# Start addresses modulo 256 of the split weights and of the streamed tiles, in a two-block fp32 network

## The reference

```python
h = rms_norm(x, norm1_g) @ w_in                      # 2048 -> 6176
x = x + concat([gla(h), windowed_attention(h)]) @ w_out
xt = rms_norm(x, norm2_g); idx, gates = topk(xt @ w_query, sub_keys)
x = x + sum_k(gates * gelu(expert_down[idx] . xt) * expert_up[idx])
for i in range(2):
    u, z = split(rmsnorm(x) @ w_in_2[i])             # 2048 -> 2 x 4096
    y = (pool_mixer(u) if i == 0 else rglru(conv(u))) * silu(z)
    x = x + rmsnorm(y @ w_out_2[i])                  # 4096 -> 2048
    x = x + rmsnorm((p[i] @ w_ple[i]) * sigmoid(rmsnorm(x) @ w_ple_gate[i]))
```

## Time and profile before

| | |
|---|---|
| median of the timed runs | 3753.89 us (3752.56 to 3755.21, 2 runs) |
| the profiled execution | 3742.33 us, span 3741.0 us |
| granted TensorE clock, mean of the profiled execution | 0.974 of full speed |
| busy: PE, DVE, ACT, POOL | 94%, 64%, 43%, 13% of the span |
| moved by DMA | 668.69 MB, 179 GB/s on average |

### The profile page before, as it was taken

The page is one execution under the profiler, slowest core; times in us unless marked ns, Lnnn a source line. Parts: engine busy times, 40 slices in busy tenths (PEclk is TensorE's granted clock), DMA queues, the critical chain, the costliest instruction groups (busy, mean ns, idle before and its releaser), DMA issues.

```text
span 3741.0 us, 67022 instructions
## 1 busy us (share of the span) xinstructions
PE 3532.1 (94%) x29266; PEld 3474.5 (93%) x29266; DVE 2396.2 (64%) x3293; ACT 1624.0 (43%) x1770; POOL 478.9 (13%) x420
## 2 busy tenths in 40 slices
PE   7999899999899998999999999999998798988987
PEld 7899899999899998999999899999998798988987
DVE  5676579874445556555555777777446777876465
ACT  3444333454444444544344543333444354555343
POOL 1000100397920000000000100000004200000013
PEclk9999999999999999999999999999998799999989
DMA  5434455455456666555666645555553344444533
GB/s 203 147 136 158 144 207 181 181 192 193 185 205 210 210 210 169 203 197 192 208 209 210 162 172 192 192 192 194 190 181 136 115 170 159 174 164 164 186 124 136
DMA packets 140388, 668.69 MB, mean 179 GB/s; under 512 B 10752, under 2 KB 60672, under 8 KB 78528
## 3 DMA queue, kind: packets, MB, share of 16 engines
q1 hardware_dynamic: 103184, 622.65, 48.1%
q10 hardware_dynamic: 36912, 41.75, 3.3%
HBM read 643.39 MB, written 20.97 MB: 178 GB/s over the span
## 4 chain that ended last, share of the span: by engine, by line
PE 77%; DVE 14%; ACT 5%; issue 4%; DMA 1%; POOL 0%; SPq 0%; ACTq 0%; DVEq 0%
PE PS L441 24%; PE PS L442 24%; PE PS L443 24%; DVE WL L1313 4%; ACT WH L887 3%; PE PS L701 1%; DVE A L1333 1%; DVE UCS L1900 1%; DVE A L1331 1%; DVE CO L1660 1%; DVE OO L1820 1%; DVE EE L1848 1%; ACT XT L1056 0%; DMA RAW<-in_w_in 0%; DVE XT L1822 0%
## 5 line engine op out<-in xcount | busy, mean ns | idle before, releaser
L1313 DVE TENSOR_TENSOR WL<-RAW,WH 128x2048 fp32r<-128x2048 f32 (+2 forms) x653 | 1359.9, 2083 | 943.3 <-ACT WH L887 942.6
L441 PE MATMUL PS<-A,WH 128*128 128x256 f32 x5648 | 1621.1, 287 | 100.0 <-DVE WL L1313 59.4
L442 PE MATMUL PS<-A,WH 128*128 128x256 f32 x5648 | 1590.6, 282 | 0.0
L443 PE MATMUL PS<-A,WL 128*128 128x256 f32 x5648 | 1590.3, 282 | 0.0
L887 ACT ACTIVATE WH<-RAW 128x2048 fp32r<-128x2048 f32 (+2 forms) x653 | 1136.6, 1743 | 851.5 <-PE PS L443 820.7
L441 PEld LDWEIGHTS PS<-A,WH 128*128 128x128 f32 x5648 | 1083.0, 192 | 132.2 <-issue 79.4
L442 PEld LDWEIGHTS PS<-A,WH 128*128 128x128 f32 x5648 | 1083.7, 192 | 3.9 <-issue 2.9
L443 PEld LDWEIGHTS PS<-A,WL 128*128 128x128 f32 x5648 | 1084.6, 192 | 0.0
L441 PE MATMUL PS<-CO,WH 128*128 128x256 f32 x2048 | 578.0, 282 | 30.8 <-DVE CO L1660 29.3
L443 PE MATMUL PS<-CO,WL 128*128 128x256 f32 x2048 | 575.0, 281 | 0.0
L442 PE MATMUL PS<-CO,WH 128*128 128x256 f32 x2048 | 574.2, 280 | 0.0
(11 more groups left out here) (236 smaller groups left out, 3180.9 us busy)
## 6 DMA issues: line engine op xcount, KB each, us to landing
RAW<-in_w_in SPq DMA_DIRECT2D x177, 1024.0 KB, 4.8
RAW<-in_peer_down SPq DMA_DIRECT2D x128, 1024.0 KB, 4.8
RAW<-in_peer_up SPq DMA_DIRECT2D x128, 896.0 KB, 5.0
RAW<-in_w_out SPq DMA_DIRECT2D x80, 1024.0 KB, 4.7
RAW<-in_w_gate SPq DMA_DIRECT2D x32, 1024.0 KB, 4.7
RAW<-in_w_query SPq DMA_DIRECT2D x16, 1024.0 KB, 4.8
gates_away<-XT ACTq DMA_DIRECT2D x16, 1024.0 KB, 4.0
RAW<-in_peer_up SPq DMA_DIRECT2D x16, 1024.0 KB, 11.0
```

The lines of the kernel that those rows point to most:

```text
L441: e.matmul(ps, wh, x[:, k, 0, :], start=first, stop=False, skip_group_check=True)
L442: e.matmul(ps, wh, x[:, k, 1, :], start=False, stop=False, skip_group_check=True)
L443: return e.matmul(ps, wl, x[:, k, 0, :], start=False, stop=last, skip_group_check=True)
L1313: ins = e.tensor_tensor(WL[:, s, cs], RAW[:, r, cs], WH[:, s, cs].bitcast(F32), ALU.subtract)
```

## The change

WH and WL are no longer one tile of three places each but six tiles. A new helper, `put_at`, places each at a given value modulo 256; where that is no multiple of 32 it places a tile that begins a few elements earlier and uses it from there on. The 64 bytes that were left out ahead of RAW are gone, and what follows the weights moves by 352 bytes. `block`, `hi` and `lo` index the lists.

```diff
     place["at"] += 64
     A = put("A", [128, KD, 2, T], FR)
-    place["at"] += 64
     RAW = put("RAW", [128, NRAW, 2048])
-    WH = put("WH", [128, NSPL, 2048], FR)
-    WL = put("WL", [128, NSPL, 2048], FR)
+
+    def put_at(name, phase):
+
+        place["at"] += (phase - place["at"]) % 256
+        skip = place["at"] % 32 // 4
+        place["at"] -= 4 * skip
+        return put(name, [128, 2048 + skip], FR)[:, skip:skip + 2048]
+
+    WH, WL = [None] * NSPL, [None] * NSPL
+    WH[0], WH[1] = put_at("WH0", 0), put_at("WH1", 64)
+    WL[0], WL[1] = put_at("WL0", 64), put_at("WL1", 64)
+    WH[2], WL[2] = put_at("WH2", 80), put_at("WL2", 80)
...
-        wh, wl = WH[:, s, b * 128:b * 128 + 128], WL[:, s, b * 128:b * 128 + 128]
+        wh, wl = WH[s][:, b * 128:b * 128 + 128], WL[s][:, b * 128:b * 128 + 128]
...
-        ins = e.activation(WH[:, s, q * n:q * n + n], RAW[:, r, q * n:q * n + n], ACT.Copy)
+        ins = e.activation(WH[s][:, q * n:q * n + n], RAW[:, r, q * n:q * n + n], ACT.Copy)
...
-        ins = e.tensor_tensor(WL[:, s, cs], RAW[:, r, cs], WH[:, s, cs].bitcast(F32), ALU.subtract)
+        ins = e.tensor_tensor(WL[s][:, cs], RAW[:, r, cs], WH[s][:, cs].bitcast(F32), ALU.subtract)
```

## The result

The changed kernel takes 3796.28 us (3795.13 to 3797.44, 2 runs) against 3753.89 before: 1.0113 times as long, interval 1.0069 to 1.0156. It is slower by 1.1%; 3689 was forecast.

What follows compares the result with a forecast made beforehand. TensorE's matmul spacing was taken as the bound. From the 3753.9 us median, 56 us plus 16 us came off, giving 3682; with a tenth of matmuls still slow the gain was 65 us, 3689, range 3620 to 3800.

Steps and rivals of the forecast that it cites:

- What bounds the kernel: Whole kernel: limited by how fast matmuls follow one another, with TensorE busy 94% of the 3741.0 us span.
- The reading that the distance decides: All block matmuls: stream start relative to weights decides possible spacings; 192 allows 113.3 and 117.77 ns, 64 only the slow one.
- Step 1: Block matmuls: the new stream-minus-weights distances, 80 to 192, were all priced at 113.3 ns.
- The bounds: Spacing limits for the unseen distances: 108.5 ns from transposes below, 117.77 ns as the longest unbroken spacing above.
- Step 2: Matmuls gaining on the path: 56 us from 12,566 slow ones plus 16 us from broken stages; 72 us, bounds 56 to 103.
- the third for the broken stages: Stages where TensorE waits: 10,530 matmuls could gain 0 to 47 us; a third was taken, 16 us.
- Steps 3 to 5: High/low splits stay covered, RAW's move costs 0, small tiles at 32 or 160 cost 0, with 7 us kept in range.
- R3: Rival, chance 0.11: 112 and 128 behave as 64, A loses its fast spacing; +39 us, 3793.
- R4: Rival, chance 0.11: weight load and moving read collide at mixed or 16-byte distances, another 4.45 ns step; +126 us, 3880.
- R1: Rival, chance 0.23: restarts set the spacing, or new distances are slow as often as old; 3754, give or take 12.

Runs made afterwards that it cites:

- distances alone: Bare kernel without the network: 512 stretches of 48 matmuls over all pairs of weight and stream starts in 16-byte steps; 113.3 ns at distance 192.

## Why the prediction was wrong

- **What bounds the kernel** held: TensorE's spacing. Nothing else moved, and 61 us more of busy TensorE became 53 us of span.
- **The reading that the distance decides** held; it is now shown (distances alone; everything 64 further; all streams at 192).
- **Step 1 failed: "I take 113.3, because it is the nearest row to a distance that is no longer 64."** The trace showed two distances, and nothing in it ordered the others. I treated 64 as a bad exception and everything else as good. It is the reverse: 192 is one of two good ones (112 the other, and only with weights at even multiples of 16), and the other distances have medians from 115.8 to 120.2 ns. A, which had the 192, now has 128 in place 1 and 112 with weights at 80 in place 2, and in the measurement of distances these cost 118.6 and 120.0 ns against 113.3; the other streams went from 64 (117.8) to 96 (120.0) in place 1 and to 80 (118.1) in place 2. In the kernel that is 3.6 ns more for each matmul on A and 1.0 for each other one, where 4.45 ns less were priced for every long one. The bounds were too narrow as well: "no longer spacing holds in any unbroken stretch" is true of the trace and says nothing about pairs that it does not hold.
- **Step 2 was right in size.** It priced all at 113.3 with 72 us off the median, 3682; the kernel that brings nearly all there is 69 us below the one before beside it, at 3682.4. That the two times agree to a microsecond is luck: the third for the broken stages was a choice, and the starting medians differ by 2 us. The step also says that DVE is busy two thirds or less in the unbroken slow windows but for 512 to 706; from 1470 to 1516 it is busy 41.79 of 46 us, which bears on 2 us of the sum.
- **Steps 3 to 5 (splits, RAW, small tiles at no cost)** held: busy times and landing are unchanged, the kernel with the weights' starts alone has the whole loss, the one with small tiles and streams alone none.
- **R3** named what happened, that A loses its short spacing, and gave 3793 against the measured 3796. Its reason ("112 and 128 behave as 64 does") is nearly right: they behave worse, by 1 to 2 ns, and the high parts of place 0, still at 192, lost it too, because the low parts between them had moved to another distance. That last I had not thought of: I counted place 0 as half kept. Of R4, a step beyond 117.8 is real as well, with 1 to 2 ns in place of 4.45, but not only at mixed or 16-byte distances (96 with all weights at one even start gives 120.0), and its collision of two reads is not shown.
- **R1** has a part of the truth: at 192 with weights at 0 the distance leaves the choice open, 12 to 12 in 24 stretches begun after a short idle, and in the kernel it is made without one too (the alternation of place 0). It fits that the executions of the kernel before lie up to 36 us apart over all these measurements (3733 to 3769), and those of the kernel with weights at 16 and all streams at 208 under 5 us. But the time of the changed kernel is not R1's: it lost the short spacing in every chunk of A.
- The Trainium skill's rule ("SBUF — State Buffer", "Who interferes with whom") that TensorE never waits on anyone is about other engines, and no run here speaks against it: the spacings come out the same with no other engine at work. What the prediction drew from it and from the two independent read ports, that addresses could cost nothing, does not hold: 113.3 to 120 ns follow from the starts alone. What collides, the two reads of TensorE or something behind them, no run here shows; that cause stays open.
- By the Trainium skill, "TensorE: Matmul & The Clock Gate", "Wait — 56ns, not 53.3ns?", 109.2 ns would be the estimate for 256 columns. None of the starts tried, in steps of 4 bytes with weights at 0, went below 113.3.

## What to carry to other kernels

When TensorE is the bound and its matmuls follow without a wait, divide an unbroken window by its count: equal instructions with different spacings are worth a measurement of starts. Measure the map in a bare kernel before placing tiles; two points of it are no ground for the other fourteen, and one run gave all of them. Then place every streamed tile and every weight buffer on purpose, at starts that gave the short spacing in every stretch and not only in half of them, high and low parts measured together, and read the addresses after rounding; a slip of 32 bytes in one tile cost most of 21 us here.

## What the runs showed of the hardware that was not expected

- The spacing of fp32r matmuls (128 weight columns, 256 streamed) depends on the starts of both operands in SBUF modulo 256: medians of 113.3 to 120.2 ns on multiples of 16 bytes (single stretches up to 123.5), up to 124 ns off them, all at the clock's level of 2.4 GHz.
- Two spacings (113.3 and 117.8) can both be stable at one pair of starts, and 2688 matmuls on end kept one of them: 113.3 in the kernel before, 117.8 in the one with everything 64 further. Where the starts change from chunk to chunk, the choice can change with them, with TensorE never idle (the low part of place 0 back at 0). What makes the choice no run shows. With weights at an odd multiple of 16 and distance 192, all 64 stretches measured had the short one.
- Mixing starts between consecutive weight loads (0 for two, 64 for the third) gives 118.3 with the stream at 192, where the first alone gives 113.3 or 117.8 and the second 118.7.
